# Eleven blocks of constant matmuls put into TensorE's waits in a three-block transformer kernel

## The reference

```python
def reference(x, c, ...):
    x = first_block(x, c, ...)    # mixer "first", then moe_ffn ("moe")
    x = second_block(x, c_2, ...) # mixer "second"
    return third_block(x, c_3, ...)

def third_block(x, c, ...):
    for layer in range(2):
        h = modulate(x, norm_mix_g[layer], sh_m, sc_m)   # RMS norm, scale, shift
        y = even_mixer(h, ...) if layer % 2 == 0 else odd_mixer(h, ...)
        x = x + g_m * y
        h = modulate(x, norm_ffn_g[layer], sh_f, sc_f)
        x = x + g_f * conv_glu_ffn(h, ...)
    return rmsnorm(x, final_g)
```

## Time and profile before

| | |
|---|---|
| device time, median of 3 runs | 2708.84 us (2707.24 to 2713.38) |
| the profiled execution, its device time | 2711.11 us |
| its span in the profile | 2709.1 us |
| mean granted clock of TensorE over the span | 0.923 |
| TensorE matmul busy | 2322.5 us, 86% of the span |
| VectorE busy | 866.7 us, 32% |
| ScalarE busy | 397.2 us, 15% |
| HBM traffic | 241 GB/s over the span |

### The profile page before, as it was taken

The page is one execution under the profiler, slowest core; times in us unless marked ns, Lnnn a source line. Parts: engine busy times, 40 slices in busy tenths (PEclk is TensorE's granted clock), DMA queues, the critical chain, the costliest instruction groups (busy, mean ns, idle before and its releaser), DMA issues. The chain is left out here.

```text
span 2709.1 us, 24757 instructions
## 1 busy us (share of the span) xinstructions
PE 2322.5 (86%) x9700; PEld 1345.9 (50%) x9700; DVE 866.7 (32%) x1718; ACT 397.2 (15%) x795; POOL 116.0 (4%) x81
## 2 busy tenths in 40 slices
PE   3978689988899888888869989878779998988998
PEld 2544434333333333333337678645648763646873
DVE  5536412221122111111236443643356301232301
ACT  1021211111111111111112311112221001221100
POOL 1000000000000000110000000000300000000000
PEclk9977689999999999999979998889889998989999
DMA  9552567899989999999976720555236443323441
GB/s 329 201 186 93 191 248 266 341 413 412 396 327 375 411 392 412 411 408 410 399 294 243 254 78 16 188 207 195 93 124 232 172 164 107 137 75 109 161 157 47
DMA packets 213260, 655.46 MB, mean 242 GB/s; under 512 B 8502, under 2 KB 13166, under 8 KB 196548
## 3 DMA queue, kind: packets, MB, share of 16 engines
q1 hardware_dynamic: 209840, 646.11, 63.0%
q0 software_dynamic: 1712, 3.60, 0.4%
q10 hardware_dynamic: 1540, 3.42, 0.3%
HBM read 652.05 MB, written 1.05 MB: 241 GB/s over the span
## 5 line engine op out<-in xcount | busy, mean ns | idle before, releaser
L1303 PE MATMUL ps<-w,XE 128*64 128x512 f32 x1536 | 360.5, 624 | 61.0 <-DMA w<-in_w_gate_up 54.2
L713 PE MATMUL ps<-HF,w 128*128 128x256 f32 x1408 | 312.0, 385 | 1.1 <-ACT HF L686 1.1
L713 PEld LDWEIGHTS ps<-HF,w 128*128 128x128 f32 x1408 | 271.3, 193 | 42.4 <-issue 3.2
L1303 PEld LDWEIGHTS ps<-w,XE 128*64 128x64 f32 x1536 | 125.6, 143 | 282.5 <-issue 275.8
L1333 DVE TENSOR_TENSOR T<-ps,BB 128x512 f32<-128x512 f32 x64 | 44.3, 692 | 642.0 <-PE ps L1303 642.0
L552 DVE SCALAR_TENSOR_TENSOR AUX<-w,CS,AUX 128x512 f32<-128x512 f32 x252 | 189.5, 752 | 8.9
L713 PE MATMUL ps<-HT,w 128*128 128x256 f32 (+1 forms) x656 | 153.8, 394 | 4.8 <-DVE dqk L2017 3.7
L1374 PE MATMUL ps<-GR,AT 128*64 128x512 f32 x256 | 125.0, 646 | 33.7 <-DMA AUX<-in_w_down 33.3
L729 PE MATMUL ps<-w,AF 128*128 128x512 f32 x352 | 151.6, 593 | 1.8 <-DVE AF L2609 1.8
L729 PE MATMUL ps<-w,HT 128*128 128x512 f32 (+1 forms) x352 | 149.6, 581 | 1.1 <-ACT HT L686 1.1
L713 PEld LDWEIGHTS ps<-HT,w 128*128 128x128 f32 (+1 forms) x656 | 126.9, 196 | 27.2 <-issue 6.2
(11 more groups left out here) (553 smaller groups left out, 2573.7 us busy)
## 6 DMA issues: line engine op xcount, KB each, us to landing
w<-in_w_gate_up SPq DMA_DIRECT2D x96, 2048.0 KB, 15.7
w<-in_w_down SPq DMA_DIRECT2D x32, 2048.0 KB, 18.7
w<-in_ada_w SPq DMA_DIRECT2D x24, 2048.0 KB, 8.0
w<-in_ffn_w_in SPq DMA_DIRECT2D x20, 2048.0 KB, 8.0
w<-in_w_in SPq DMA_DIRECT2D x17, 2048.0 KB, 10.6
GR<-in_w_gate_up SPq DMA_DIRECT2D x16, 2048.0 KB, 18.1
AUX<-in_w_gate_up SPq DMA_DIRECT2D x16, 2048.0 KB, 22.7
GR<-in_w_down SPq DMA_DIRECT2D x16, 2048.0 KB, 10.1
```

The lines of the kernel that those rows point to most:

```text
L713: ins = e.matmul(out_, w[:, k, c:c + n], HT[:, k, :], start=k == 0, stop=k == kc - 1, skip_group_check=True)
L1303: ins = e.matmul(b[j * n:j * n + n, :], FM.XE[:, side(x), 4 * kh + k, j * n:j * n + n], ring.tile(512, 1024, "gu", ex_, h, kh, x[0])[:, k, ...
```

## The change

A new helper `busy_pe(e, n)` takes the next PSUM bank and issues n matmuls of 128x512 into it, the identity as weights and the first 512 columns of the constant table as the moving operand, both float32 and in SBUF since the start. Nobody reads the bank. It is called at eleven places, with 83 matmuls in all (166 records in the trace): 9 in each of the six norms after the first, and 3, 3, 6, 7 and 10 inside second, even and odd. Line numbers behind the helper are 13 or more higher in the changed kernel (L672 is L685 there).

```diff
+    def busy_pe(e, n):
+
+        n_busy[0] += 1
+        b = bank.take(e, "busy", n_busy[0])
+        for _ in range(n):
+            ins = e.matmul(b, ident, CT[:, 0:512], start=True, stop=True, skip_group_check=True)
+        ins.then_inc(*pe())
+        pe.leave("bank", "busy", n_busy[0])
+
     def norm_pe(e, f, tag):
+        if tag != "first":
+            busy_pe(e, 9)
         e.wait_ge(*at(tag, "xn"))
         turn_pe(e, tag, lambda t, k: f.XN[:, t, cols(k)], 8)
@@ inverse_pe
         W = (W5[t], W6[t])
+        if s == 0 and t == 0:
+            busy_pe(e, 3)
         if s == 0:
@@ even_pe
             ins.then_inc(*pe("eo", t))
+        busy_pe(e, 6)
         e.wait_ge(*at("LK"))
@@ odd_pe
         pe.leave("w", "gates")
+        busy_pe(e, 7)
         b = bank.take(e, "ccm")
         e.wait_ge(*at("igcm"))
@@ odd_pe
         e.wait_ge(*at(("hno", 1), "out"))
+        busy_pe(e, 10)
         turn_pe(e, "OTo", lambda t, k: FO.O[:, t, cols(k)], 8)
```

More of the change, by code:

```diff
@@ L661, in norm_dve @@
         turned_dve(e, tag, f.HT, 8, lambda k: MOD[:, 2 * slot + 1, k:k + 1], lambda k: MOD[:, 2 * slot, k:k + 1])
+    n_busy = [0]
+    def busy_pe(e, n):
[5 more added lines that the diff above has]
+        pe.leave("bank", "busy", n_busy[0])
     def norm_pe(e, f, tag):
+        if tag != "first":
+            busy_pe(e, 9)
         e.wait_ge(*at(tag, "xn"))
```

## The result

| | before | changed |
|---|---|---|
| median of the runs | 2709.16 us (2703.64 to 2713.38, 8 runs) | 2720.03 us (2716.90 to 2728.92, 8 runs) |
| ratio to before | 1 | 1.0044 [1.0030, 1.0057] |
| profiled execution, and its span | 2711.11 us, 2709.1 us | 2719.45 us, 2717.4 us |
| mean granted clock of the span | 0.923 | 0.940 |

A forecast was written before the change was run, and what follows sets the result against it. Time was taken to be bound on TensorE's own line, by waits, turns and cold projections at stage boundaries. The places' nets of +9.6 us plus 2.5 for falls gave +12 on 2708.8, 2721 us, range 2710 to 2733.

The forecast's parts named there:

- moe: Norm at moe's start: cold block overshoots 4.5 us, turn gives back 1.55 and router 2.5, net +0.5 us.
- second: Norm at second's start: cold block overshoots 5.5 us, warmer turn and projections give back 3.85, net +1.6 us.
- even: Norm at even's start: cold block overshoots 5.5 us, only the turn gains, 1.55, net +3.9 us.
- OTo: Behind the wait for OO: ten cold matmuls, 11.05 us, all overshoot; 3.5 us come back, net +7.55 us.
- falls: Warm blocks that meet a fall of the clock anyway, one or two of ten gains: 2.5 us added.
- The blocks wait for the join: At the joins, blocks wait for the join, not for the end of TensorE's own work; no size of its own.
- Prices of the blocks: Nine matmuls take 10.2 us from a cold start and 7.8 us warm; OTo's ten take 11.05 us cold.
- quick clock: Rival: full clock from each block's first matmul, six cold blocks lose 2.35 us each, 2703 us; chance 0.07.
- The turn: Transposes of the normed input behind a block: 1.80 us warm instead of 3.65; with evictions 1.55 us less.
- The clock falls again behind each turn: Rival: gains behind the turns vanish, 15.2 us, and even's projections lose 2.3; +27 us, 2736 us; chance 0.10.
- Identity matmuls don't raise the clock: Rival: every block runs cold, 15.7 us for nine, and nothing is gained; about +94 us, 2803 us; chance 0.03.
- The overshoot is partly absorbed: Rival: waits for weights in moe and at second's output absorb up to 5 us; +7 us, 2716 us; chance 0.08.

The follow-up runs named there:

- experiment 8: Kernel before plus one block only, 12 dead matmuls ahead of OTo's wait for OO: 2704.39 us against 2709.92, ratio 0.9978.
- experiment 3: Kernel before plus one block only, 10 dead matmuls behind OTo's wait for OO: 2720.01 us against 2710.68, ratio 1.0037.
- experiment 5: Changed kernel with its blocks behind joins cut to the room there, 38 matmuls instead of 83: 2679.06 us, ratio 0.9895 to the kernel before.
- experiment 2: Kernel before plus only the blocks that start warm, at LK, ffn0, odd, the gates and ffn1: 2706.7 us against 2710.68, ratio 0.9985.
- experiment 9: Kernel before, no dead matmuls, GpSimd's broadcasts of the first bias rows waiting until VectorE has written PG: 2706.42 us against 2707.94, ratio 0.9993.
- experiment 7: Kernel before plus one block only, 36 dead matmuls behind the join to moe: 2726.4 us against 2709.92, ratio 1.0056.
- experiment 4: Kernel before plus 98 dead matmuls, placed ahead of the joins and waits and sized by the idle time: 2676.51 us against 2710.68, ratio 0.9875.
- experiment 1: Kernel before plus only the cold blocks behind joins, at moe, second, second c, OT2 and even: 2714.7 us against 2710.68, ratio 1.0016.
- experiment 6: Against experiment 4, 14 matmuls instead of 19 ahead of second's join and 6 more in even: 2671.92 us, ratio 0.9859 to the kernel before.

## Why the prediction was right

2721 us were forecast and 2720.03 measured; +12 us forecast and +10.9 measured. By its steps, with each place's net read from the two traces (start of the same matmul, changed against before):

| place | forecast | trace |
|---|---|---|
| moe | +0.5 | +2.2 |
| second | +1.6 | +2.1 |
| second c | +0.6 | +0.1 |
| OT2 | +1.1 | +1.5 |
| even | +3.9 | +5.0 |
| LK | 0 | 0 |
| ffn0 | -1.0 | -1.0 |
| odd | -1.95 | -2.1 |
| gates | -2.3 | -2.2 |
| OTo | +7.55 | +8.0 |
| ffn1 | -0.4 | -0.5 |

The places sum to +13.1, where the prediction had 9.6 and 2.5 more for falls. A later wait behind ffn0 cost 1.2 us more, and three stretches without any block moved too: +2.3 at the start-up ahead of the first block, -4.3 in moe's body, -3.9 at second's output. That makes 13.1 + 1.2 + 2.3 - 4.3 - 3.9 = 8.4, where the spans differ by 8.3. At second's output most of it is the clock: the kernel before ran 6.5 us of it at 0.50 (first row), which cost some 3.3 us, and in the changed kernel the clock stayed at 1.00 from 1725 to 1792 us (second row).

```profile
1756.00:1762.50 6.50, 5.22 (x6) 2.19 (x7) 4.00 (x7) 0.00 (x0) 0.00 (x0) 0.50 1.05 388
1725.00:1792.00 67.00, 59.37 (x228) 39.69 (x226) 42.86 (x78) 7.73 (x12) 0.00 (x0) 1.00 0.91 325
```

So the steps hold, and the hit by one microsecond is in part luck. None of these stretches was forecast; they took 4.7 us off. The prediction also read every wait from one execution: five traces with no block at second have that place 2.3 us shorter than the kernel before has it, and the start-up is 1.9 to 6.1 us longer in every other trace than in it. The stated lower end, 2712, is lower than its own terms give (2721 - 2.4 - 2.5 - 1 = 2715).

*The blocks wait for the join.* Right. L670 starts 0.2 to 0.4 us after the last row of X, and 5.9, 13.5, 10.2 us of idle stand ahead of it at moe, second and even; 11.48 us at OTo. All the rest hangs on this step; experiment 8 against 3 shows its price at OTo.

*Prices of the blocks.* A cold block of nine was put at 10.2 us and took 10.02, 10.73 and 9.83; a warm one at 7.8 took 7.96. OTo's ten were put at 11.05 and took 11.84. The stretches of the changed kernel:

```profile
1407.60:1418.30 10.70, 10.69 (x20) 4.67 (x21) 1.58 (x3) 2.41 (x5) 2.36 (x4) 0.74 1.05 383
1798.50:1808.40 9.90, 9.86 (x20) 4.43 (x21) 1.58 (x3) 2.60 (x5) 0.50 (x1) 0.81 0.00 0
1812.10:1828.10 16.00, 16.00 (x67) 13.64 (x68) 12.33 (x20) 0.81 (x3) 0.00 (x0) 0.89 0.37 132
2025.60:2033.50 7.90, 7.90 (x20) 3.55 (x21) 1.66 (x4) 3.83 (x6) 0.00 (x0) 1.00 0.69 262
2420.90:2432.70 11.80, 11.80 (x22) 5.06 (x23) 0.00 (x0) 0.00 (x0) 0.00 (x0) 0.74 0.00 0
```

A mean of 0.74 to 0.81 over a block that ends warm is a start at the lower level, 1.2 GHz; 1.00 at ffn0 is a block at the upper level throughout. So the rival of the *quick clock* is refuted: its point of decision was a cold time under 1.5 us, and the cold time is 2 x 0.26 x 10.7 = 5.6 us at second and 2 x 0.19 x 9.9 = 3.8 at even.

*The turn.* Put at 1.55 us less with its evictions; the matmuls' part is 1.91 for 3.65. At moe the turn's gain was 1.7 us. In experiment 5 it was 1.5 there. The page's rule (the Trainium skill, TensorE: Matmul & The Clock Gate, Part 4: PE-mode transpose), by which the full clock doesn't engage for transposes, is not borne out here: the turns run at the upper level, 1.91 us for 3.65, and the projections behind the turn at second start at the warm pace.

*The clock falls again behind each turn.* Refuted as a rule, and right at two places. At even the 64 records of L726 took 15.75 us where they take 14.05 at second, in the stretch of 0.89 above: 1.7 us of the 5.0. At moe the mean clock was 0.57 over the 11.1 us from the router's first matmul on. The allowance of 2.5 us for falls anywhere holds even's. The fall at even is nothing that blocks bring: experiments 2, 3 and 9 have it there without one, and the place costs them 1.3 to 1.7 us.

*moe.* Mis-sized, +2.2 for +0.5. The overshoot was 4.3 us for 4.5 and the turn gave its 1.7, but the router's 32 records took 5.68 us for 7.01: 1.3 us gained where I counted 2.5, and the gather behind ran colder than before.

*Identity matmuls don't raise the clock.* Refuted by every block: 15.7 us were to be expected for nine.

*The overshoot is partly absorbed.* Not in moe's body: experiment 7 put 23.9 us into its start, and 22.6 of them were there at its end. The 4.3 us that the changed kernel gained in moe say little: the same stretch is 5.5 us longer to 4.6 us shorter than in the kernel before in the traces of the ten experiments, and none has an edit in it.

What the experiments add is the step that the prediction took as given and did not question: how many matmuls it takes. Experiment 5 gave two or three to the same cold joins, which fit into the wait, and second's start cost 5.8 us less than with nine. The nine ran 4 to 6 us past the wait at each cold join, more than their warm clock gave back. Not the idea, but the size and the place of the blocks made the change slow.

## What to carry to other kernels

A block of dead matmuls (whose result nobody reads) belongs ahead of the wait whose idle time it is to fill, never behind it: at OTo, ten behind the last wait cost 9.3 us and twelve ahead of it gained 5.5. Behind a join it can stand only where another wait follows, and only as long as that one (experiment 5). Its length is the idle time that the trace shows, at the pace that the clock has there, less a microsecond of slack, since what runs over is paid (3.9 us at second in experiment 4). So placed and sized, and with eight blocks more, the same function made this kernel 41 us faster instead of 11 slower. And a single trace is one draw: where the clock falls differs between executions of the same code, so a gain at one place has to be held against several traces without the edit before it is called the edit's.

## What the runs showed of the hardware

**VectorE under GpSimd's broadcast.** Two products of 128x256 take 0.43 us each alone and 2.41 and 2.36 us under PARTITION_BROADCAST (two records, 4.69 us together); each of them ends about 0.1 us after one of the two records. In experiment 1 the first product started within 0.01 us of the broadcast and took 0.43 us, and the two records took 4.99. The Trainium skill (SBUF — State Buffer, Who interferes with whom) has the two engines share a port pair as an exclusive lock, and a VectorE instruction with two SBUF inputs contend with a GpSimd instruction that reads SBUF. The trace agrees for these products: the wait is that of one broadcast record for each product, not a share of bandwidth.

**A recursion with small gaps loses the clock, and not always the same way.** In second c TensorE waits 0.7 to 1.3 us between short groups. One piece of it, 23.7 us long in the kernel before at a mean clock of 0.57 (2 x 0.43 x 23.7 = 20.4 us at the lower level), is the same in the changed kernel and in experiments 2, 6, 7, 8 and 9. In experiments 3 and 4 it took 20.1 and 20.3 us at 0.75, which is 10 us at the lower level, in experiment 5 18.9 us at 0.82 (7 us), and in experiment 1 17.5 us at 0.90 (3.5 us). Up to there, experiment 3 has the code of the kernel before and experiment 1 that of the changed one. The whole recursion was 6.2 to 8.5 us shorter in experiments 1, 3 and 5, about as much as several of the differences measured here, and a reason to read a small difference only from many runs.

**A turn alone can bring the clock up.** In experiment 8 TensorE was idle for 18.22 us ahead of second's turn, the turn ran at the lower level for all of its 3.64 us, and the projections behind it took the warm 14.05. In the kernel before the same projections took 16.34 us behind the same turn.
